# A two-block transformer kernel: the opening modulation matrix taken in two column halves, with products of the first two weight units between them

## The reference, cut to what matters

```
ada = c @ w_ada + b_ada                  # w_ada is 1024 x 6144
shift1, scale1, gate1, shift2, scale2, gate2 = split(ada, 6)
h    = rmsnorm(x, g_norm1) * (1 + scale1) + shift1
proj = h @ w_in                          # the next products of 1024 rows
q_f, k_f, v_f, f_logit, q_d, k_d, v_d, q_i, k_i, w_i, gates = split(proj)
x = x + gate1 * (sigmoid(gates) * attention branches) @ w_out
h2 = rmsnorm(x, g_norm2) * (1 + scale2) + shift2
x = x + gate2 * (relu(h2 @ w_mlp1)**2 @ w_mlp2)
```

## Time and profile before

| | us |
|---|---|
| median of 3 runs | 1375.69 (1374.22 to 1376.92) |
| span of the profiled execution, first to last instruction | 1373.2 |
| median less that span | 2.5 |
| TensorE busy in the span | 1329.0 (97%) |

### The profile page before, as it was taken

How to read it: one execution, slowest core, us unless ns; L and a number is a source line. 1 busy time by engine, 2 the same in 40 slices (tenths; PEclk the granted TensorE clock), 3 DMA queues, 4 the chain that set the end, 5 groups by cost and what they waited for, 6 DMA issues and landing times.

```text
span 1373.2 us, 16276 instructions
## 1 busy us (share of the span) xinstructions
PE 1329.0 (97%) x6233; PEld 1096.0 (80%) x6233; DVE 824.8 (60%) x1119; ACT 657.0 (48%) x1048; POOL 80.5 (6%) x116
## 2 busy tenths in 40 slices
PE   2999999999999999999999999999999999999997
PEld 2788877888888888888877888888888888888885
DVE  5686767867565654457447554556644576755454
ACT  2666655553444543445656444444444444544342
POOL 3501100100000100001001000001000010100000
PEclk9999999999999999999999999999999999999999
DMA  9757654459355655655624754647555555565551
GB/s 337 256 201 247 231 211 169 169 184 325 134 200 168 215 184 203 195 184 173 206 113 159 228 194 155 204 165 241 188 199 184 184 202 197 185 214 184 186 194 50
DMA packets 156716, 268.37 MB, mean 195 GB/s; under 512 B 9477, under 2 KB 101717, under 8 KB 155616
## 3 DMA queue, kind: packets, MB, share of 16 engines
q1 hardware_dynamic: 148896, 239.43, 50.6%
q0 software_dynamic: 7744, 27.91, 6.0%
HBM read 266.21 MB, written 1.07 MB: 195 GB/s over the span
## 4 chain that ended last, share of the span: by engine, by line
PE 90%; DVE 3%; DMA 3%; ACT 2%; issue 1%; POOL 0%; SPq 0%; DVEq 0%; ACTq 0%; POOLq 0%
PE UP L685 18%; PE UP L687 17%; PE UP L686 17%; PE Y L685 10%; PE Y L687 10%; PE Y L686 10%; PE TB L759 4%; DMA RAW<-in_w_in 1%; DVE WL L1451 1%; DMA X<-in_x 1%; PE Y L791 1%; PE Y L798 1%; ACT WH L1088 0%; DMA RAW<-in_ffn_w_gu 0%; PE TB L835 0%
## 5 line engine op out<-in xcount | busy, mean ns | idle before, releaser
L1451 DVE TENSOR_TENSOR WL<-RAW,WH 128x1024 fp32r<-128x1024 f32 (+1 forms) x442 | 507.9, 1194 | 180.7 <-ACT WH L1088 174.6
L1088 ACT CAST WH<-RAW 128x1024 fp32r<-128x1024 f32 (+1 forms) x442 | 430.0, 1032 | 211.0 <-PE Y L687 117.5
L685 PE MATMUL UP<-WH,AH 128*128 128x512 f32 (+1 forms) x1136 | 459.4, 404 | 1.2 <-DVE AL L1457 0.5
L687 PE MATMUL UP<-WH,AL 128*128 128x512 f32 (+1 forms) x1136 | 444.2, 391 | 0.0
L686 PE MATMUL UP<-WL,AH 128*128 128x512 f32 (+1 forms) x1136 | 442.5, 390 | 0.0
L687 PEld LDWEIGHTS UP<-WH,AL 128*128 128x128 f32 x1136 | 214.1, 188 | 46.1
L685 PEld LDWEIGHTS UP<-WH,AH 128*128 128x128 f32 x1136 | 214.5, 189 | 43.8 <-issue 2.6
L686 PEld LDWEIGHTS UP<-WL,AH 128*128 128x128 f32 x1136 | 215.0, 189 | 40.5 <-issue 0.2
L685 PE MATMUL Y<-WH,HH 128*128 128x512 f32 (+1 forms) x496 | 193.9, 391 | 0.0
L687 PE MATMUL Y<-WH,HL 128*128 128x512 f32 (+1 forms) x496 | 191.6, 386 | 0.0
L686 PE MATMUL Y<-WL,HH 128*128 128x512 f32 (+1 forms) x496 | 191.4, 386 | 0.0
(11 more groups left out here) (228 smaller groups left out, 905.3 us busy)
## 6 DMA issues: line engine op xcount, KB each, us to landing
RAW<-in_ffn_w_gu SPq DMA_DIRECT2D x176, 512.0 KB, 4.8
RAW<-in_ffn_w_down SPq DMA_DIRECT2D x80, 512.0 KB, 4.1
RAW<-in_w_mlp SPq DMA_DIRECT2D x64, 512.0 KB, 4.2
RAW<-in_w_in SPq DMA_DIRECT2D x38, 512.0 KB, 5.4
PIECE<-in_w_ada POOLq DMA_DIRECT2D x32, 512.0 KB, 5.4
RAW<-in_a_w_in SPq DMA_DIRECT2D x24, 512.0 KB, 4.6
WADA<-in_w_ada SPq DMA_DIRECT2D x7, 1024.0 KB, 10.0
RAW<-in_w_out SPq DMA_DIRECT2D x8, 512.0 KB, 3.9
```

The lines of the kernel that those rows point to most:

```text
L685: pe.matmul(dst, ah, wh, start=first, stop=False)
L687: return pe.matmul(dst, al, wh, start=False, stop=last)
L1088: act.copy(WH[:, u % 2, q * n:(q + 1) * n], raw_half(u, q // 2)[:, (q % 2) * n:(q % 2 + 1) * n]).then_inc(wh_done, 1)
L1451: ve.tensor_tensor(WL[:, u % 2, o], raw_half(u, q // 2)[:, (q % 2) * n:(q % 2 + 1) * n], WH[:, u % 2, o].bitcast(F32), ALU.subtract).then_ ...
```

## The change

The opening slices are taken in two column halves: `WADA` now holds eight slices of 128 rows by 2 x 512 columns. For each half, slice 0 is multiplied by c on TensorE (`ada_first`), slices 1 to 6 are added on VectorE, slice 7 comes and is added in two pairs of channel tiles, and TensorE's sums follow for each pair. Between the halves TensorE multiplies the first four k-tiles of units 0 and 1, unit 0 into the banks `UP` and unit 1 into the banks `Y[1]`. SP issues x first, then the first half of unit 0, then the first half of the matrix, the first half of unit 1, the second half of the matrix, and the second halves of units 0 and 1, for which unit 1 has `RAW2`, which lies over slices 0 and 1 of `WADA`. The three small tables (b_forget, rel_bias, onehot) move from POOL's queue to SP's, behind the second half of unit 0. The table matmul `rev_row(0)` moves from the opening to after the first block of unit 2, and its transfers follow on POOL. ScalarE also makes the modulated values (MOD) of the second half, which VectorE made. The two logarithms come together after both absolute values and exponentials. `MODULATION` takes (0, 0, 2, 2) pieces at u = 0 to 3 in place of (2, 0, 1, 1). The splitting of unit 2 is spread among the forget gates and the index scores.

```
-MODULATION = (2, 0, 1, 1, 3, 3, 3, 3, 3, 3, 2)
+MODULATION = (0, 0, 2, 2, 3, 3, 3, 3, 3, 3, 2)
-    keys = [("col",), ("tab", 0)]
+    keys = [("col",)]
-    keys.extend([("qi", 0), ("qi", 1), ("qf", 0), ("F",), ("qf", 1), ("kf", 0), ("kf", 1),
+    keys.extend([("qi", 0), ("qi", 1), ("qf", 0), ("F",), ("qf", 1), ("tab", 0), ("kf", 0), ("kf", 1),
+OPENING = {(u, q): i + 1 for i, (u, q) in enumerate(
+    (u, 2 * part + q) for part in range(2) for u in range(2) for q in range(2))}
-        WADA = over("WADA", [P, 4, 2 * D], 0)
+        WADA = over("WADA", [P, KT, 2, HALF], 0)
+        RAW2 = over("RAW2", [P, 2048], 0)
 def up_bank(u, tok):
-            return UP[WIDE_NO[u, tok] % 2]
+            return Y[1][tok] if u == 1 else UP[WIDE_NO[u, tok] % 2]
 # SP
+            def ada_half(h):
+                for k in range(KT - 1):
+                    if h:
+                        sp.wait_ge(*((wada_read, 1) if k == 0 else (wada_used, k)))
+                    sp.dma_start(WADA[:, k, :, :], wada[:, k, :, h * HALF:(h + 1) * HALF]).then_inc(in_wada[k], 16)
+                if h:
+                    sp.wait_ge(acc_done, 2)
+                for pair in range(2):
...
+            for tok in range(TOK):
+                sp.dma_start(X[:, tok, :], t["x"][0, tok * P:(tok + 1) * P, :]).then_inc(in_x[tok], 16)
+            raw_load(0, 0)
+            ada_half(0)
+            raw_load(1, 0)
+            ada_half(1)
+            raw_load(0, 1)
...
+            sp.wait_ge(wada_read, 2)
+            sp.wait_ge(wada_used, KT - 1)
+            raw_load(1, 1)
 # TensorE
-            rev_row(0)
+            ada_first(0)
             for tok in range(TOK):
                 pe.wait_ge(xhat_done, tok + 1)
                 chain_turns("h", tok, Z)
+            ada_columns(0)
+            opening(0, range(TOK), range(4))
+            ada_first(1)
+            opening(1, range(TOK), range(4))
+            ada_columns(1)
+            opening(0, range(TOK), range(4, KT))
+            opening(1, (0,), range(4, KT))
+            from_tmp(("qi", 0), 3)
+            opening(1, (1,), range(4, KT))
+            from_tmp(("qi", 1), 3)
+            from_tmp(("qf", 0), 4)
+            (F and the index scores, then u = 2, and behind its first block rev_row(0))
 # ScalarE
+            round_unit(0, (0, 1))
             (x scaled, h taken)
+            mod_highs(0)
+            mod_highs(1)
+            round_unit(1, (0, 1))
+            round_unit(0, (2, 3))
+            mod_highs(2)
+            mod_highs(3)
+            round_unit(1, (2, 3))
...
+            round_unit(2, (0,))
...
+            index_in(0)
+            query_in(0)
+            index_in(1)
+            round_unit(2, (1,))
+            query_in(1)
 # VectorE
+            split_unit(0, (0, 1))
+            ada_sums(0)
+            scales(0)
+            modulated(0)
+            scales(1)
+            mod_lows(0)
+            modulated(1)
+            mod_lows(1)
+            split_unit(1, (0, 1))
+            ada_sums(1)
+            split_unit(0, (2,))
+            scales(2)
+            split_unit(0, (3,))
+            scales(3)
+            mod_lows(2)
+            mod_lows(3)
+            split_unit(1, (2, 3))
```

More of the change, by code:

```diff
@@ L451, in raw_landed @@
             n = u + 1 - (u > last_bout)
[L452 removed]
+            return raw_in[half], 32 * (n - 1 if u > 1 else n)
         def emptied(b):
@@ L508, in _ @@
-            for u, (name, kind, width, kts) in enumerate(UNITS):
+            wada = t["w_ada"].rearrange("(k p) n -> p k n", p=P)[:, :, 0:2 * D].rearrange(
+                "p k (a n) -> p k a n", a=2)
+            def ada_half(h):
[6 more added lines that the diff above has]
+                for pair in range(2):
+                    s = slice(pair * 2 * P, (pair + 1) * 2 * P)
+                    sp.dma_start(WADA[:, KT - 1, :, s],
+                                 wada[:, KT - 1, :, h * HALF + pair * 2 * P:h * HALF + (pair + 1) * 2 * P]
+                                 ).then_inc((in_wada[KT - 1], in_last)[pair], 16)
@@ L517, in _ @@
[L517 to L548, removed]
@@ L549, in _ @@
-                    for dd, ss in parts:
-                        sp.dma_start(dd, ss).then_inc(raw_landed(u, half)[0], 16)
+                    raw_load(u, half)
             for tok in range(TOK):
@@ L642, in _ @@
             gp.dma_start(KF[96:97, :, :], FTN[:, :]).then_inc(in_forget, 16)
+            table(0)
+            pieces(2, 4)
+            table_read(0)
+            gp.wait_ge(wl_done, quarter_no(1, 3))
             for h in range(2):
@@ L1198, in _, with mod_highs @@
                     taken(("h", tok, h), XT[:, 4 * h:4 * h + 4, tok * P:(tok + 1) * P], HALF)
-            def mod_highs(h):
-                act.wait_ge(scale_done, h + 1)
-                for k in range(4 * h, 4 * h + 4):
+            def mod_highs(pair):
+                act.wait_ge(scale_done, pair + 1)
+                for k in (2 * pair, 2 * pair + 1):
                     act.activation(AH[:, k, :], XT[:, k, :], ACT.Identity, bias=SHIFT[:, k:k + 1],
                                    scale=SCALE[:, k:k + 1]).then_inc(mod_high, 1)
-            round_unit(0, (0, 1))
+                    if pair >= 2:
+                        act.activation(MOD[:, k, :], XT[:, k, :], ACT.Identity, bias=SHIFT[:, k:k + 1],
+                                       scale=SCALE[:, k:k + 1]).then_inc(mod_done, 1)
@@ L1211, in _ @@
+            query_in(0)
+            index_in(1)
+            round_unit(2, (1,))
+            query_in(1)
+            taken_heads(("qf", 0), QF, slice(0, P))
+            for h in range(NI):
+                act.wait_ge(idx_done, h + 1)
+                if h >= 1:
+                    act.wait_ge(r_used, h)
+                act.activation(PR[:, 0, :], IDX[h][:, 0:REV], ACT.Relu, scale=DH ** -0.5).then_inc(r_done, 1)
+                if h < 2:
+                    round_unit(2, (h + 2,))
             att = 0
@@ L1587, in modulated, with scales @@
+            def scales(pair):
+                p = pair % 2
+                ve.wait_ge(ada_done, pair + 1)
+                q = slice(2 * pair, 2 * pair + 2)
+                step(ve.tensor_tensor(SCALE[:, q], Y[0][p][:, 2:4], COLS[:, 8 + 2 * pair:10 + 2 * pair], ALU.add))
+                ve.tensor_tensor(SHIFT[:, q], Y[0][p][:, 0:2], COLS[:, q], ALU.add)
+                ve.tensor_tensor(SCALE[:, q], SCALE[:, q], COLS[:, 16 + 2 * pair:18 + 2 * pair], ALU.mult
                                  ).then_inc(scale_done, 1)
-                ve.wait_ge(scale_done, h + 1)
@@ L1589, in modulated, with mod_lows @@
-                for k in range(4 * h, 4 * h + 4):
+            def modulated(pair):
+                ve.wait_ge(scale_done, pair + 1)
+                for k in (2 * pair, 2 * pair + 1):
                     ve.tensor_scalar(MOD[:, k, :], XT[:, k, :], SCALE[:, k:k + 1], SHIFT[:, k:k + 1],
                                      ALU.mult, ALU.add).then_inc(mod_done, 1)
-            def mod_lows(first, end):
-                for k in range(first, end):
+            def mod_lows(pair):
+                for k in (2 * pair, 2 * pair + 1):
```

332 lines of the change are left out of this document (182 added, 150 removed).

## The result

The changed kernel takes 1377.35 us (median of 19 runs) against 1375.39 for the kernel before (19 runs on the same chips): ratio 1.0013, 95% interval 1.0007 to 1.0019. Of all the runs in this document one, of a_tab_sp, was slow (3804 us) and stands in no ratio. The changed kernel is 2 us slower, where 7.5 us faster was forecast, and the time lies outside the range of 1364.0 to 1374.5.

The account below looks back on a forecast made before the run. TensorE, busy 97% of the span, was taken as the bound, with time to win at 0 to 66 us. 9.5 sooner less 0.7, 1.1 and 0.2 gave 7.5 us: 1368.2 us, range 1364.0 to 1374.5.

Parts of the forecast that it names:

- Given back: After unit 2 starts: 0.7 us for rev_row and 1.1 for a wider gap lost from the 9.5 us lead.
- the pause: TensorE's 0.88 us gap before 99.53, ahead of the head's values at u = 4; forecast to grow by 1.1 us.
- Rival (c): Units 2 and 3: late raw halves of unit 3 make TensorE wait; 5.5 us back, about 1373.7; chance 0.10.
- First columns: Opening: with half the matrix landed at 374 GB/s, first dense matmul at 24.1, 13.0 us sooner than 37.15.
- Between the halves: VectorE's second-half sums to 37.0; TensorE through first k-tiles of units 0 and 1 at 38.3, last column sums to 40.0.
- Second columns: Unit 0's last k-tiles, paced by ScalarE's MOD, end at 45.2; unit 1's blocks end at 48.8 and 52.4.
- Unit 2: After turned queries, F and scores (4.2 us), unit 2 starts at 56.6 in place of 66.07: 9.5 us sooner.
- The wait of 2.38 us: TensorE's wait before the turned query, after unit 1's last matmul; forecast to vanish.
- Rival (a): Opening transfers reach only 313 GB/s with 2 KB rows and more requests; gain 4.0, time 1371.7; chance 0.10.
- Rival (b): TensorE's clock drops between halves, during column sums from 38.3 to 41.3; 2.8 us, time 1371.0; chance 0.13.
- Rival (d): TensorE stays at 1.2 GHz through the whole opening; unit 2 starts at 68.4, time 1379.8; chance 0.07.

Follow-up runs that it names:

- a_tab_sp: Changed kernel with the 1 MB table read issued on SP's queue behind unit 5's second raw half, not on POOL's ahead of both: 1370.81 us, ratio 0.9971.
- a_tab_late: Changed kernel with only the 1 MB table read moved later, behind pieces 4 and 5 and the split of unit 5: 1371.89 us, ratio 0.9974.
- a_tab_early: Changed kernel with the table matmul back in the opening and the 1 MB table read issued near 52 us, not 81: 1372.11 us, ratio 0.9976.
- a_late_pieces: a_early_pieces with the table read issued behind the split of unit 5 in place of near 52 us: 1371.71 us, ratio 0.9972.
- a_pieces: Changed kernel with one piece each at u = 2 and 3 in place of two, and two more at u = 10: 1374.27 us, ratio 0.9997.
- a_tab_other: Changed kernel with the same-sized table read taken from a weight matrix, at the same moment and queue (bias then wrong): 1376.26 us, ratio 1.0009.
- a_early_pieces: a_tab_early with no pieces at u = 2, two at u = 3, one more each at u = 7 and 8: 1368.62 us, ratio 0.9950.
- a_pieces2: a_early_pieces with one piece at u = 3 in place of two and four at u = 6 in place of three: 1367.94 us, ratio 0.9946.
- a_first_late: a_early_pieces with ada_first(1) moved behind the first four k-tiles of both unit 0 and unit 1: 1369.76 us, ratio 0.9959.

## Why the prediction was wrong

**The step that failed** is a term that stood at nothing: the move of `table_read(0)`. It was told in the change and had no price in the sum. "Given back" has only "Small tables on SP, POOL's memsets in new order, `RAW2`: at nothing. Their cover is 10 us of idle transfers after 46 us", and for the pause "the gap grows by 1.1. Its bounds are 0 and 1.8". The idle transfers after 46 us were cover for the old place. `table(0)` cannot be issued before ScalarE has taken the turned row at u = 2 (72.87), `pieces(2, 4)` stands ahead of the read on POOL and waits for VectorE's eight rounds and two pieces, and so the read came out at 81.20, 1.6 us ahead of unit 5's first raw half and 3.9 us ahead of the second, the one transfer that I had named as critical. I followed the wait of SP (`wl_done`) and not POOL's.

The gap grew by 7.45 in place of 1.1. Its parts can be read off: the raw half took 5.33 us longer and started 0.5 longer after VectorE's split of unit 4, and the two engines' places give the other 1.6. Measured from the start of unit 2, VectorE ended that split 3.7 us later than before (forecast 1.8) and TensorE came 2.0 later (forecast 0.7). Both terms were too small, and by luck their difference, 1.6, was near the 1.1. With the read out of the way the gap grew by 1.3 to 1.4 (a_tab_sp, a_tab_late).

**The whole miss.** At the third score the forecast leaves a lead of 7.7 us, and the arrears were 3.6. Of these 11.3 us 6.4 are the pause beyond the 1.1. Another 1.8 are the half clock behind it, for which the sum had nothing (from the end of the pause to the third score 7.38 us, 5.58 before). 1.8 are the later start of unit 2, and 1.3 the way from there to the second score. By the medians, moving the read alone gives back 5.2 to 6.5 of the 9.2 us between 1377.35 and 1368.2.

Rival (c) had the right place, and a price of 5.5 back by a late half of unit 3. Its mechanism was another, and the pause and the half clock behind it cost 9.25.

**Point by point.**

- *First columns*: 24.1 forecast, 25.19 measured. 374 GB/s was near: 387 in 25 to 30 us. VectorE's sums ended at 21.38 for 21.4. The column sums ended at 24.34 for 21.8: of the earlier trace rows's 16 in 3.29 us two belong to each matmul of the program (TensorE's timeline before has 32 for 16 matmuls), so a pair has eight and not four, 1.8 us, and the second pair's stand behind the first's. Over half of that was got back, since the first pair was scaled and modulated meanwhile.
- *Between the halves*: VectorE ended at 37.98 for 37.0, never waiting for a transfer after the first slice of the half. TensorE reached the column sums at 40.8 for 38.3; 1.7 of that is the half clock in unit 1's products (7.1 us for 5.5).
- *Second columns*: tiles paced by MOD at 0.5 for each of its instructions, as said, but the clock was at half there too, and unit 0's four k-tiles took 5.3 us for 3.9, ending 3.9 late.
- *Unit 2*: 58.41 for 56.6, and in four of the kernels above 55.8 to 56.4. That it was only 1.8 late is owed to two terms that were too high: unit 1 followed without waits (5.8 us for 7.2), and the turns, F and the scores ran at full clock (3.5 for 4.2).
- *The wait of 2.38 us* went, as said.
- *Until the second score*: 2.0 given back for the 0.7 of `rev_row` alone; taking `rev_row` away (a_tab_early) gave 0.6, and the rest is small waits of TensorE for `WL` in unit 2 (0.26 at 63.4) and others that I did not separate.
- *Rival (a)*, slower transfers, did not happen, nor did requests of 512 KB pay for themselves one by one.
- *Rival (b)*, a fall of the clock, happened twice, one of them at a place I had not named, in `ada_first(1)`.
- *Rival (d)* did not: in the opening half clock covers 3.4 us twice, and the start.

Two kernels come out at the forecast, 1368.62 and 1367.94 for 1368.2. That is partly luck and no proof of the sum. They keep the halves, but they also have `rev_row` back in the opening and fewer pieces at u = 2 and 3, so that the pause to which the sum gave 1.1 us is gone. The kernels in which only the read is moved came to 1370.8 to 1372.1: within the range, 2.6 to 3.9 above the forecast.

## What to carry to other kernels

When a change moves an instruction past another on a queue, follow its transfers to the time at which they will really be issued, by what stands ahead of them on that queue, and set that time beside the issue of each transfer that someone waits for. Here a megabyte that nobody wanted soon held up the wanted halves by several microseconds when it was issued ahead of them, though on another queue than theirs, and not at all behind them, on either queue. A lead won at the start of a pipeline is kept only if the next transfers on the chain are issued sooner too, so price the first wait behind the lead anew.

## What the runs showed of the hardware

**A fall of the clock in mid-opening comes and goes between profiled executions of the same opening.** In after, a_tab_early, a_tab_late, a_tab_sp and a_late_pieces the clock was at half for 3.4 us, beginning between 33.2 and 34.4 us, and unit 2 started at 58.2 to 58.9. In a_pieces, a_tab_other, a_early_pieces and a_pieces2 it stayed at full from 28.3 to 29.0 on until 41.9 to 42.6, and unit 2 started at 55.8 to 56.4, though nothing ahead of 42 us differs in the instructions of after, a_pieces and a_tab_other. This is a window of a_early_pieces, with a clock of 1.00:

```profile
29.10:42.50 13.40, 12.93 (x79) 10.98 (x78) 11.68 (x19) 3.77 (x7) 0.00 (x0) 1.00 1.00 326
```

The same two microseconds of single-column products thus went with a fall or with none. With it unit 1's first products took 7.13 us (after), without it 5.58 (a_pieces and a_early_pieces), which is 1.55 of the 2.3 us in the start of unit 2. Most of the rest lies ahead of it: where the fall came, the clock had come up later, between 29.8 and 30.9 us. What decides it, no run here shows. In a_first_late the clock also came up late, at 30.0, but dense products followed, and there was no fall at 33.

**The clock's share shows in the spread of runs, too.** Of a_tab_sp's ten runs the four with a mean granted clock of 0.989 took 1373.5 to 1374.0 us, the six with 0.991 to 0.996 took 1368.4 to 1370.8. A part of that may be what follows the pause at u = 4 in the profiled executions. From its end to the third score a_tab_sp, with the clock at half from 95.6 to 102.4, took 8.74 us after a pause of 2.14; a_tab_late, with the clock up, took 5.57 after one of 2.26.

**Requests of 512 KB in rows of 2 KB run at 387 GB/s when queued** (25.2 to 30.1 us after), for 418 with 1 MB and rows of 8 KB. The Trainium skill, "DMA: Bandwidth & Descriptors", Bandwidth, asks for 1 MiB or more; the trace gives a loss of 7% for half of that, row length included.
